# Block 1's routed experts: one step per expert, 4 KB token rows, four places for weights, two sums instead of three

## The reference

```python
scores = jax.nn.sigmoid(xt @ w_router)                  # 512 tokens, 64 experts
...                                                     # 4 of 8 groups kept, then the 8 best experts of each token
wts = wts / jnp.sum(wts, axis=-1, keepdims=True) * 2.5
...
yb = (silu(xe @ w_gate[e]) * (xe @ w_up[e])) @ w_down[e]   # 1024 -> 256 -> 1024, for each expert's tokens
routed = segment_sum(yb * slot_w, slot_tok)
shared = (silu(xt @ w_sh_gate) * (xt @ w_sh_up)) @ w_sh_down
x = x + g2 * rmsnorm(routed + shared)
```

## Time and profile before

| what | value |
|---|---|
| median of 3 runs | 3191.98 us (3186.73 to 3194.73) |
| the profiled execution | 3193.44 us |
| its span, first to last instruction | 3191.7 us |
| granted TensorE clock, mean | 0.942 |
| PE busy | 2779.7 us, 87% |
| DVE, ACT, POOL busy | 929.3, 460.0, 501.5 us |
| L1888, gate and up, x3072 passes | 356.4 us busy |
| L1902, down, x768 passes | 187.1 us busy |
| L2205, accumulating transfers, x96 | 1588 ns each on POOL |
| L2178, gathers, x96 | 1050 ns each on POOL |
| L1794 and L1797, loads of an expert | 2048 KB and 1024 KB |

### The profile page before, as it was taken

How to read it: one execution, slowest core, us unless ns; L and a number is a source line. 1 busy time by engine, 2 the same in 40 slices (tenths; PEclk the granted TensorE clock), 3 DMA queues, 4 the chain that set the end, 5 groups by cost and what they waited for, 6 DMA issues and landing times.

```text
span 3191.7 us, 36733 instructions
## 1 busy us (share of the span) xinstructions
PE 2779.7 (87%) x15269; PEld 1338.4 (42%) x15269; DVE 929.3 (29%) x1541; ACT 460.0 (14%) x1007; POOL 501.5 (16%) x383
## 2 busy tenths in 40 slices
PE   5999699989989899988999498685998898888887
PEld 2644566744435454444445233443332232223232
DVE  2043556531123511111111476843111111111112
ACT  2011233201012111111111201430000000000001
POOL 0001134312001133433434101301000000000000
PEclk8899899989989999999999799797999999999999
DMA  5020154442122599997999420034999999999996
GB/s 229 27 79 0 55 160 148 146 155 104 75 95 104 194 351 387 370 364 286 361 371 371 145 89 23 24 146 159 421 421 421 421 421 421 421 421 421 422 421 286
DMA packets 127325, 792.94 MB, mean 248 GB/s; under 512 B 21795, under 2 KB 22179, under 8 KB 56761
## 3 DMA queue, kind: packets, MB, share of 16 engines
q1 hardware_dynamic: 102328, 743.86, 57.9%
q0 software_dynamic: 23008, 37.81, 4.9%
q10 hardware_dynamic: 1824, 8.91, 0.7%
HBM read 768.91 MB, written 38.86 MB: 253 GB/s over the span
## 4 chain that ended last, share of the span: by engine, by line
PE 55%; DMA 28%; DVE 9%; issue 4%; ACT 3%; POOL 1%; ACTq 0%; POOLq 0%; SPq 0%; DVEq 0%
DMA arena<-in_w_down 12%; PE b L2991 10%; DMA yd<-arena 9%; PE b L1452 5%; PE b L1888 4%; PE b L492 4%; DMA arena<-h2d,arena 3%; PE b L3026 3%; PE b L494 3%; PE b L2479 2%; PE b L1902 2%; PE b L633 2%; PE b L1516 2%; PE b L1470 2%; DVE arena L2525 2%
## 5 line engine op out<-in xcount | busy, mean ns | idle before, releaser
L2991 PE MATMUL b<-arena 128*64 128x512 f32 x2048 | 457.6, 604 | 18.1 <-DMA arena<-in_w_up 7.8
L1888 PE MATMUL b<-arena 128*64 128x256 f32 x3072 | 356.4, 384 | 5.4 <-DMA arena<-in_w_gu 4.2
L3006 PE MATMUL b<-arena 128*64 128x512 f32 x1024 | 244.2, 602 | 57.2 <-DMA arena<-in_w_down 57.0
L2991 PEld LDWEIGHTS b<-arena 128*64 128x64 f32 x2048 | 156.0, 139 | 315.9 <-issue 276.6
L1888 PEld LDWEIGHTS b<-arena 128*64 128x64 f32 x3072 | 213.5, 137 | 117.2 <-issue 5.4
L2205 POOL DMA_INDIRECT yd<-arena x96 | 152.5, 1588 | 344.8 <-ACT arena L1986 113.7
L1902 PE MATMUL b<-arena 128*64 128x512 f32 x768 | 187.1, 608 | 0.9 <-issue 0.7
L2161 DVE TENSOR_TENSOR arena<-arena,b 128x128 f32<-128x128 f32 x96 | 27.8, 290 | 519.7 <-ACT arena L1979 481.9
L1452 PE MATMUL b<-arena 128*128 128x512 f32 x384 | 167.0, 596 | 9.1 <-DMA arena<-in_w_in 9.1
L3006 PEld LDWEIGHTS b<-arena 128*64 128x64 f32 x1024 | 65.0, 136 | 235.8 <-DMA arena<-in_w_down 136.2
L3098 DVE TENSOR_TENSOR arena<-arena,b 128x512 f32<-128x512 f32 x32 | 20.6, 686 | 463.7 <-PE b L2991 463.7
(11 more groups left out here) (479 smaller groups left out, 3382.7 us busy)
## 6 DMA issues: line engine op xcount, KB each, us to landing
arena<-in_w_gu SPq DMA_DIRECT2D x65, 2048.0 KB, 9.7
arena<-in_w_gate SPq DMA_DIRECT2D x128, 1024.0 KB, 27.0
arena<-in_w_up SPq DMA_DIRECT2D x128, 1024.0 KB, 26.1
arena<-in_w_down SPq DMA_DIRECT2D x128, 1024.0 KB, 24.5
arena<-in_w_dn SPq DMA_DIRECT2D x65, 1024.0 KB, 11.9
arena<-in_w_mod SPq DMA_DIRECT2D x80, 512.0 KB, 3.7
arena<-in_w_in SPq DMA_DIRECT2D x19, 2048.0 KB, 8.0
arena<-yd SPq DMA_DIRECT2D x12, 512.0 KB, 8.6
```

The lines of the kernel that those rows point to most:

```text
L1888: x = e.matmul(ps[i % 2][64 * j:64 * j + 64, 0:256], XGT[i % 2][:, k % 4, (k // 4) * 64:(k // 4) * 64 + 64], GUB[place_of(w)][:, k, j * 25 ...
L2991: x = e.matmul(ps[b + c][64 * hf:64 * hf + 64, :], XS[q % 2][:, kb, (n % 2) * 64:(n % 2) * 64 + 64], w[:, u * 512:(u + 1) * 512], start=(k ...
L3006: x = e.matmul(ps[4][64 * hf:64 * hf + 64, :], H[:, c * 4 + j, hi * 64:hi * 64 + 64], w[:, i * 1024 + hf * 512:i * 1024 + hf * 512 + 512], ...
```

## The change

Block 1's expert loop has 64 steps, one per expert, in the same order of pairs. An even step is an expert with two blocks (`whole`): 128 tokens, each a row of 4 KB. An odd step is an expert with one block: 64 tokens of 4 KB on 64 partitions.

- A whole step's products use the whole array: 8 products of 512 columns for gate and up, 4 of 512 for down, 8 transposes of tokens, 2 of the hidden block. A half step keeps the two tiles; its tokens come from 64 partitions in 8 transposes of 64 columns.
- A gather or accumulation moves 128 rows of 4 KB in a whole step and 64 in a half step. There are 128 such transfers instead of 192.
- There are four places for tokens instead of six, three for results (of 4 KB) instead of four, four for weights instead of three. The fourth place for weights lies where the routing's tables were, and its first load waits for them.
- There are two arrays of sums instead of three. Even steps add to the first, odd steps to the second. The transfer of step i waits for that of step i-2. Combine reads and adds two arrays.
- The down products of a step fill two banks of PSUM and wait for ACT's two copies of the step before; the tokens' transposes fill two banks in a whole step.
- The overflow loop moves to step 33; it handles 64 rows of 4 KB at a time.

The core of the diff:

```diff
-    self.yd = [dram(f"yd{i}", [1024, 512], F32) for i in range(3)]
+    self.yd = [dram(f"yd{i}", [512, 1024], F32) for i in range(3)]
...
-MID = 48
+MID = 33
+SUMS = 2
...
-    order = [0, *range(1, blocks[MID][0]), None, *range(blocks[MID][0], 65)]
+    order = [*range(MID), None, *range(MID, N)]
...
     def place_of(w):
-        return (number[w] + 2) % 3
+        return number[w] % 4
     def freed(e, n, kind):
-        w = order[n - 3]
...
+        if n == 2:
+            e.wait_ge(*mm.at("s_" + kind, 3))
+        elif n == 3:
+            e.wait_ge(*mm.at("table", 31))
+        elif n > 3 and order[n - 4] is None:
+            e.wait_ge(o["end"], 16)
+        elif n > 3:
+            e.wait_ge(*mm.at(kind, order[n - 4]))
...
+    def gate_up(e, i):
+        g = GUB[place_of(i)]
+        e.wait_ge(*came_gu[place_of(i)].at(i))
+        e.wait_ge(*dve.at("xt", i))
+        if i >= 2:
+            e.wait_ge(*dve.at("hid", i - 2))
+        for k in range(8):
+            if whole(i):
+                x = e.matmul(ps[i % 2][:, :], XGT[i % 2][:, hs(k)], g[:, k, :], start=(k == 0), stop=(k == 7))
+                continue
+            for j in range(2):
+                x = e.matmul(ps[i % 2][64 * j:64 * j + 64, 0:256], XGT[i % 2][:, k * 64:k * 64 + 64],
+                             g[:, k, j * 256:(j + 1) * 256], start=(k == 0), stop=(k == 7), skip_group_check=True)
+    def down(e, q):
+        e.wait_ge(*came_dn[place_of(q)].at(q))
+        e.wait_ge(*act_.at("hidT", q))
+        if q >= 1:
+            e.wait_ge(*act_.at("y", q - 1))
+        for j in range(2):
+            for c in range(2):
+                if whole(q):
+                    x = e.matmul(ps[4 + c][:, :], HDT[q % 2][:, hs(j)], d[:, j, c * 512:(c + 1) * 512], start=(j == 0), stop=(j == 1))
+                else:
+                    x = e.matmul(ps[4][64 * c:64 * c + 64, :], HDT[q % 2][:, 64 * j:64 * j + 64],
+                                 d[:, j, c * 512:(c + 1) * 512], start=(j == 0), stop=(j == 1), skip_group_check=True)
...
     def tokens_T(e, i):
-        for c in range(4):
-            x = e.transpose(p[:, hs(c)], XG[i % 6][:, hs(c)], K.ident)
+        for k in range(8):
+            if whole(i):
+                x = e.transpose(ps[6 + k // 4][:, hs(k % 4)], XG[i % 4][:, hs(k)], K.ident)
+            else:
+                x = e.transpose(ps[6][:, k * 64:k * 64 + 64], XG[i % 4][0:64, hs(k)], K.ident[0:64, 0:64])
...
+    def weighted(e, q):
+        r, y = ranks[q], Y[q % 3]
+        e.wait_ge(*mm.at("dn", q))
+        if q >= 3:
+            e.wait_ge(*yout[q % 3].at(q - 3))
+        for c in range(2):
+            rs = slice(64 * c, 64 * c + 64)
+            dst, src, w = (y, ps[4 + c], WS) if whole(q) else (y[0:64], ps[4][rs], WS[rs])
+            x = e.activation(dst[:, c * 512:(c + 1) * 512], src[:, :], ACT.Copy, scale=w[:, r:r + 1])
...
         for i in range(N):
-            if i == MID - 3:
+            if i == MID - 2:
...
-            gather(e, i + 6)
+            gather(e, i + 4)
             e.wait_ge(*act_.at("y", i))
-            if i >= 3:
-                e.wait_ge(*yout[(i - 3) % 4].at(i - 3))
-            e.indirect_dma_start(K.yd[i % 3], off(GI.bitcast(U32)[:, b:b + 1]), Y[i % 4], None, bounds_check=1023,
+            if i >= SUMS:
+                e.wait_ge(*yout[(i - SUMS) % 3].at(i - SUMS))
+            e.indirect_dma_start(K.yd[i % SUMS], off(GI.bitcast(U32)[rows_of(i), r:r + 1]), Y[i % 3][rows_of(i), :], None, bounds_check=511,
...
-        e.tensor_tensor(YA[t], YA[t], YB[t], ALU.add).then_inc(*dve.up("part", t))
-        e.wait_ge(*dve.now())
-        e.wait_ge(*came_y[3 * t + 2].at("y", t))
-        e.tensor_tensor(YA[t], YA[t], YC[t], ALU.add).then_inc(*dve.up("sum", t))
+        e.tensor_tensor(YA[t], YA[t], YB[t], ALU.add).then_inc(*dve.up("sum", t))
```

More of the change, by code:

```diff
@@ L1715, in experts @@
     hi = K.area(K.base1 + 4096, K.keep1)
-    XG = [hi(512) for _ in range(4)]
+    XGf = hi(2048)
     ar = K.area(K.keep1)
@@ L2191, in pool @@
         all_of(e, *began, zeroed)
-        for i in range(6):
+        for i in range(4):
             gather(e, i)
```

221 lines of the change are left out of this document (108 added, 113 removed).

## The result

The changed kernel takes 3205.55 us (median of 7 runs, 3202.93 to 3208.45) beside 3191.98 for the kernel before (7 runs, 3181.50 to 3198.04) on the same chip: a ratio of 1.0047, with an interval of 1.003 to 1.0063. I had forecast 3163 and a range of 3142 to 3184. The forecast was wrong, and its sign too.

A forecast was written before the change was run, and what follows sets the result against it. The prediction took PE to bound the expert loop, with transfers close behind. From 3193.4 us it took 12.8 (PE's work), 10 (gather waits), 5.6 (fourth place) and 4.7 (combine), and added 2.8: 3163 us, range 3142 to 3184.

The forecast's parts named there:

- What bounds the kernel now: Expert loop, 1112 to 1773 us: PE sets the pace, with transfers close behind; 96 blocks make 607 of 661 us.
- PE's work: Expert loop: a pair of experts takes 18.56 us instead of 18.96; 12.8 us less over 32 pairs.
- the cheap end: Half steps' eight transposes cost no more than the four before; 27 us less in all instead of 12.8.
- Transfers: Expert loop's weights and tokens: engines' time falls from 625 to 600 us, beside a stage shortened to 635.
- the transfers stay a close second: Expert loop: 600 us of transfers stay below the stage's 635 us.
- The middle price of 3.3 us per MB: Queue q0's token transfers with 4 KB rows: taken between 2.48 and 4.05 us per MB; 136 us become 111.
- The gather waits: PE's waits for tokens' gathers in the expert loop: 10 of 15.4 us gone.
- The fourth place: One more expert's weights in store removes the weights' wait and slow product behind the overflow loop: 5.6 us less.
- What is added and combine: First gather, overflow loop and last step add 2.8 us; combine with two arrays instead of three saves 4.7 us.
- The first: Rival: transfers set the pace in the expert loop and gather waits stay; priced at 3175 us, chance 0.22.
- The second: Rival: the chain of accumulations on one sum slows the expert loop; 3214 us, chance 0.06.
- the third: Rival: half steps' transposes or switching between whole and tiled products cost PE more; 3195 us, chance 0.06.

The follow-up runs named there:

- e9: The kernel before, with the tokens permuted within each block of 64 so that they spread over the DMA engines: 3173.48 us, ratio 0.9934.
- e15: The changed kernel with half steps' gathers made as transfers of 128 rows, upper 64 out of range, rows still unevenly spread: 3209.84 us, ratio 1.006.
- the even version: The changed kernel with each step's tokens placed on other rows, so that they are dealt evenly to the 16 DMA engines: 3184.43 us, ratio 0.9961.
- e14: The changed kernel with tokens dealt evenly to engines and half steps' gathers made 128 rows wide, upper 64 out of range: 3166.77 us, ratio 0.9923.
- e3: The changed kernel with three places for weights instead of four: 3223.55 us, ratio 1.0092 to the kernel before.
- e8: The changed kernel with three sums in DRAM in turn instead of two, a third of the routed part left out: 3211.74 us, ratio 1.005.
- e1: The changed kernel with the half steps' 64 rows on partitions 64 to 127 instead of 0 to 63: 3214.17 us, ratio 1.0073.

## Why the prediction was wrong, point by point

**What bounds the kernel now: half right.** PE was busy and rarely waited. But the two windows that I read are the stage's fullest, and two between them have PE at 93 and 94%. And "the stage is PE's, with transfers close behind" was read from a mean over 16 engines. e9 moves no byte less and gains 20 us, so the kernel before already lost up to 20 us to its fullest engines (its fullest one carried 9.6 rows for a pair, the mean was 8.0). They came out as gather waits and as products at a lower clock behind them: the granted clock is 0.72 from 1280 to 1286 us, behind the wait of 2.36 us.

**PE's work: the mechanism right, the size too small.** I took 18.56 us for a pair in place of 18.96, and 12.8 us in all. A pair takes 17.92, so the term is 32 x 1.04 = 33.3. The whole steps' parts were nearly as forecast (6.96, 0.93, 3.43 and 0.37 from start to start, 11.69 in sum against 11.80). The half steps' were not: eight transposes of 64 rows take 0.65 us, next to the cheap end that I named and did not take, and one transpose of the hidden block among others takes 0.11. The nearest row by the kind of instruction was not the nearest by the size of the tile.

**Transfers: this step failed, in three terms.** The step is "the transfers stay a close second", 600 us of transfers beside a stage of 635. The runs show that the fullest engines and the stretched weights set the pace of the changed kernel's pairs.
- The middle price of 3.3 us per MB. A 2 KB accumulating packet takes 176 ns and one of 4 KB 327. Gathered rows came in 4 KB packets of 159 ns in the kernel before too, in the stretch of the earlier trace rows as well, so no row showed a gather in pieces of 2 KB and the gathers had nothing to gain. Summed over a token's packets that is 159 + 2 x 176 = 511 ns before and 159 + 327 = 486 after. Queue q0 cost 0.226 x 328/19.30 = 3.84 us per MB. Of the 25 us less that I expected for the engines' sum, 7 are left.
- The weights at an unchanged price. They cost 7.88 us for an expert instead of 7.66: 64 x 0.22 = 14 us more. Half of the gathers have 64 rows now; made 128 rows wide they give back 0.14 of the 0.22 here (e15) and 0.32 in the even version (e14). In sum 504 + 129 = 633 us where I had 600.
- The mean for the fullest engine. By an estimate from the packets, with unstretched weights (8 x (0.611 + 0.309) = 7.36 us) and 12 rows of 0.486 us it needs 2 x 7.36 + 5.8 = 20.5 us for a pair, with the mean stretched ones 21.6. PE needs 17.92. The changed kernel's pairs took 17.9 us at the loop's start, out of the weights in store, and 19.5 to 22.9 in the steady stretches. "The transfers stay a close second" should have read: they set the pace.

**The gather waits: the number near, by luck.** I had 10 of the 15.4 us gone; all went but the first step's, which grew from 6.16 to 7.27. In the changed kernel PE is late for the weights, and no gather is late behind the first step; that the one brings the other is argued, not shown, and my own reason was not put to a test. Nor did show it: their brackets name ACT's result, not an earlier accumulation, as what POOL waited for. (Over the stage POOL did wait for earlier accumulations in the kernel before, 69.8 us in 17 pieces, and 15.4 in 2 in the changed one.) e9 shows that waits fall from 15.4 to 7.9 us with even engines alone.

**The fourth place: wrong as a term.** The 4.15 us behind the overflow loop went, and the two pairs there run in 17.9 us each from the weights in store; but 56.4 us of waits for weights came elsewhere. e3 shows that without the place it would have been 14 to 18 us worse. A store only smooths; it can't help where each pair needs more transfer time than product time.

**What is added and combine: right within what can be told.** From the end of the loop to block 2's first product it is 4.0 us less, 4.7 by the forecast. The start took 2.6 us more from the first gather to the first gate and up, 1.4 by the forecast; the longer wait and the first transposes (1.97 us at a granted clock of 0.50, the lower level, behind that wait, where the same eight take 1.09 later) are the rest. The overflow wait was 8.9 us, not 16.0, and stayed between 6.7 and 16.8 through all kernels.

**The rivals.** The first, that the transfers set the pace, is what happened, yet its price, 3175, was too low: it took the engines' sum at the old cost and let the kernel lose only what I had hoped to gain. No case had the transfers' side grow dearer, though the change altered the shape of every token transfer. The second and the third fell, by e8 and by the 17.92 us.

**A check of the whole.** The forecast's loop was 661 less 28 and some added, about 635 us. With both causes removed e14 has 629.6 us, and its time is 3166.8, 4 us from the forecast. That nearness is luck: two errors cancel, PE's larger gain (33 for 12.8 us) and the 20.4 us for which it still waits for weights. What the runs show is that removing both causes takes back 38.8 us, more than the 13.6 us that the changed kernel lost. What is not settled is why gathers of 64 rows stretch packets of other transfers, and why the wide ones shrink them less in e15, where the engines are uneven. The 64 rows go to 64 partitions through 16 engines, the 128 rows of the other form to 128; whether the way into those partitions or the order of rows does it, no run here divides.

## What to carry to other kernels

A DMA share is a mean: before calling transfers second, work out the fullest engine, from which rows of each transfer are full and to which engines they go. Where tiles are filled only in part, deal the entries out so that every engine gets its part; it cost a constant table, and in the changed kernel a few table products, and gave about 20 us in either kernel. And when a change alters the shape of transfers, give the case that they become dearer a price of its own, also for the transfers that don't change.

## What the hardware showed that I had not expected

- An accumulating packet of 4 KB takes 327 ns, one of 2 KB 176, a stored or gathered one of 4 KB 159. Accumulating doubled the engine's time per byte here, and 4 KB rows gave back only 7% of what 2 KB rows took.
- A transfer of 128 rows with only the first 64 in use ran on eight engines; the same 64 rows as a transfer of 64 used all 16 (chains of eight and of four rows). In e1 it made no difference on which partitions they lay.
- One gather of 64 rows for a pair of experts went with a mean time of the weights' packets of 7.84 to 7.94 us for an expert instead of 7.56 to 7.66, two with 8.26. All kernels fit but e15 (7.74, with none).
- Eight transposes of 64 rows and 64 columns take 0.65 us, where eight full ones take 0.93.
